# Three of eight channel groups of a depthwise convolution move from VectorE to GpSimd

## The chip, the cores and the metric

The kernel runs on one core of a Trainium2 chip. The metric is the device time of one execution in microseconds (us), as the median of several runs.

## The reference

Two transformer blocks run one after the other on 256 tokens of width 2048, all in float32. The first block is the one that matters here. After a norm and a projection, half of the columns go into a gated, causal depthwise convolution of 1024 channels with 31 taps, and the others into latents for an attention of 8 heads:

```
h = rmsnorm(x, pre_mix_norm);  z = h @ w_in
a, g = split(conv_in);  u = a * sigmoid(g)
u[t, c] = conv_b[c] + sum over j < 31 of conv_w[j, c] * u[t - 30 + j, c]
u = silu(layernorm(u, conv_ln_g, conv_ln_b))
q = rmsnorm(q_lat) @ w_uq;  k, v = rmsnorm(kv_lat) @ w_ukv;  rotary parts;  attn = causal_attention(q, k, v)
mix = concat(rmsnorm(u), rmsnorm(attn)) @ w_out;  x = x + rmsnorm(mix)
x = x + rmsnorm((silu(hf @ w_gate) * (hf @ w_up)) @ w_down),  hf = rmsnorm(x)
```

The second block (window attention, gated linear attention and a convolved feed-forward net) is untouched.

## The kernel before

All weight matrices are streamed from HBM in tiles of 256 rows (two chunks of 128) by up to 512 columns, through a ring of 4 buffers. For each tile ScalarE rounds the weights to a high part (`w_hi`, line 1073), VectorE subtracts to get the low part (`w_lo`, line 1623, both inputs in SBUF), and TensorE multiplies high by high, high by low and low by high (lines 484 to 486): 12 matmuls of up to 512 columns. The rounding of a tile waits until TensorE has used the tile four places earlier; TensorE waits for `lo_ready`, which the subtraction raises. The order of work on every engine is written out by hand: `lo_upto(g)` on VectorE issues the subtractions up to tile g, and other work is put between.

The convolution has its channels on partitions, in 8 groups of 128 (`CC`), with 256 tokens in the free dimension and 30 zeros ahead of them (`uT`). Two halves of the channels become ready at two times: `u_ready`, transposes on TensorE (line 562), and copies out of PSUM on ScalarE (line 1146, `cu_free`). One tap of one group is one VectorE instruction of 128x256, `cv = uT shifted * weight + cv` (line 1729); the first also adds the bias (line 1726). There are 31 x 8 = 248. They are issued by `taps(n)`: 3 behind each of 50 tiles of the input, latent and up projections (`TILE_TAPS`), 12 behind each head of the attention (`ATTN_TAPS`), and the rest ahead of the output projection. The constant `CONV_DVE` lists the groups of each half. With eight groups, four stand in each half.

The attention of the first block has a software pipeline over heads: TensorE transposes q and k of head h+1 (`attn1_T`, lines 607 to 610), makes the scores of head h (`attn1_S`), transposes the weights of head h-1 and makes the product of head h-2. VectorE adds the mask and takes the maximum (lines 1794 to 1797), ScalarE takes exponentials (line 1209), and VectorE scales the output (line 1805). After it TensorE fills the transposed inputs of the output projection (line 500), multiplies two tiles, and then waits for the convolution (`conv_tap`, at g == 2) to sum its columns for the layer norm (line 695).

GpSimd makes constants at the start. After that it takes one power per norm, in the order `R_ORDER` ("x0" the first norm, "lat" the latents, "attn" the attention's), each when VectorE has its mean square: `rstd = ms ** -0.5` (line 465), for which ScalarE waits before it scales the projections' outputs. In the second block it also does rotary products (`rotate`, lines 453 to 458), which read two tensors of SBUF each.

Of the kernel before, what the change touches and what calls it, by code (L numbers as in the profile page):

```python
# [20 lines left out]
F32 = mybir.dt.float32  # L21
F32R = mybir.dt.float32r
I32 = mybir.dt.int32
ALU = mybir.AluOpType
# [3 lines left out]
P = 128  # L28
SEQ = 256
# [10 lines left out]
CC = CONV // P  # L40
TAPS = 31

CONV_DVE = ([0, 1, 2, 3], [4, 5, 6, 7])
TILE_TAPS, ATTN_TAPS = 3, 12
DVE_TAPS = TAPS * sum(len(c) for c in CONV_DVE)
HEADS = 8
NOPE, ROPE, VD = 128, 64, 128
# [2 lines left out]
QC, KVC = QL // P, KVL // P  # L50
# [65 lines left out]
G_AT, _n = {}, 0  # L116
# [7 lines left out]
def build(nc, a, out):  # L124
    ctx = ExitStack()
    with ctx:
# [3 lines left out]
        def overlay(tensors):  # L130

            inner = ExitStack()
            got = [inner.enter_context(nc.sbuf_tensor(n, s, d)) for n, s, d in tensors]
            inner.close()
            return got

        def sem(name):
            return ctx.enter_context(nc.semaphore(name))
# [12 lines left out]
        gains = sb("gains", [P, G_ROWS])  # L151
        convw = sb("convw", [P, TAPS * CC])
# [16 lines left out]
        y_dn, _, grow_dn = overlay([("y_dn", [P, TOK * DM], F32), ("under_grow", [P, DM], F32), ("grow_dn", [P, DM], F32)])  # L169
# [3 lines left out]
        z1, uT, cv, q1, kv1, attn1, qkT, qpeT, att1_s, att1_p, kpe, kpeT = overlay([  # L173
            ("z1", [P, TOK, Z1], F32), ("uT", [P, CC, SEQ + TAPS - 1], F32), ("cv", [P, CC, SEQ], F32),
            ("q1", [P, TOK, HEADS * QKH], F32), ("kv1", [P, TOK, DM], F32), ("attn1", [P, TOK, CONV], F32),
            ("qkT", [P, 2, 2, SEQ], F32), ("qpeT", [ROPE, 2, SEQ], F32), ("att1_s", [P, 2, 3 * P], F32),
            ("att1_p", [P, 2, 3 * P], F32), ("kpe", [P, TOK, ROPE], F32), ("kpeT", [ROPE, SEQ], F32)])
        taken = sum([TOK * Z1, CC * (SEQ + TAPS - 1), CC * SEQ, TOK * HEADS * QKH, TOK * DM, TOK * CONV,
                     4 * SEQ, 2 * SEQ, 6 * P, 6 * P, TOK * ROPE, SEQ])
        _, latT_hi, latT_lo = overlay([("under_lat", [P, taken], F32),  # L180
                                       ("latT_hi", [P, QC + KVC, SEQ], F32R), ("latT_lo", [P, QC + KVC, SEQ], F32R)])
        _, lnsq = overlay([("under_ln", [P, taken], F32), ("lnsq", [P, CC, SEQ], F32)])

        taken = TOK * Z1 + CC * (SEQ + TAPS - 1) + CC * SEQ
        _, grow_out = overlay([("under_gout", [P, taken], F32), ("grow_out", [P, DM], F32)])
        taken += TOK * HEADS * QKH
# [6 lines left out]
        taken = TOK * Z2 + 8 * NB  # L193
# [35 lines left out]
        dve_step, act_step, pool_step = sem("dve_step"), sem("act_step"), sem("pool_step")  # L229
        ms_ready, rstd_ready, sq_done = sem("ms_ready"), sem("rstd_ready"), sem("sq_done")  # L230
        u_ready, cu_ready, cu_free = sem("u_ready"), sem("cu_ready"), sem("cu_free")
        conv_tap = sem("conv_tap")
        trig_arg, trig_abs, trig_done = sem("trig_arg"), sem("trig_abs"), sem("trig_done")
        at_T, at_qk, at_S, at_max, at_exp, at_PT, at_pT, at_PV, at_out = (
            sem("at_T"), sem("at_qk"), sem("at_S"), sem("at_max"), sem("at_exp"), sem("at_PT"), sem("at_pT"),
# [173 lines left out]
        @block.gpsimd  # L409
        def _(pool):  # L410
            count = [0]

            def step(ins):
                count[0] += 1
                ins.then_inc(pool_step, 1)
                pool.wait_ge(pool_step, count[0])

            step(pool.memset(ident[:], 0.0))
            pool.affine_select(out=ident[:], in_=ident[:], compare_op=ALU.not_equal, fill=1.0, base=0,
                               pattern=[[-1, P]], channel_multiplier=1).then_inc(ident_ready, 1)  # L420
            step(pool.memset(masks[:], 0.0))
            step(pool.memset(tri[:], 1.0))

            for at, sign in ((0, 1), (2 * P, 1), (3 * P, -1)):
                step(pool.affine_select(out=masks[:, at:at + P], in_=masks[:, at:at + P], compare_op=ALU.is_ge,
                                        fill=MASKED, base=0, pattern=[[-sign, P]], channel_multiplier=sign))

            for d, (m, c) in enumerate([(-1, 1), (1, -1)]):
                step(pool.affine_select(out=tri[:, d, :], in_=tri[:, d, :], compare_op=ALU.is_ge, fill=0.0,
                                        base=0, pattern=[[c, P]], channel_multiplier=m))  # L430
                step(pool.affine_select(out=tri[:, d, 0:CHUNK], in_=tri[:, d, 0:CHUNK], compare_op=ALU.is_ge,
                                        fill=0.0, base=CHUNK - 1, pattern=[[0, CHUNK]], channel_multiplier=-1))
                step(pool.affine_select(out=tri[:, d, CHUNK:P], in_=tri[:, d, CHUNK:P], compare_op=ALU.is_ge,
                                        fill=0.0, base=-CHUNK, pattern=[[0, CHUNK]], channel_multiplier=1))
            step(pool.tensor_copy(gmask[:], tri[:]))

            step(pool.affine_select(out=gmask[:, 1, :], in_=gmask[:, 1, :], compare_op=ALU.is_gt, fill=0.0,
                                    base=0, pattern=[[-1, P]], channel_multiplier=1))
            pool.iota(posf[:, 1, :], pattern=[[P, TOK]], base=0, channel_multiplier=1,
                      allow_small_or_imprecise_dtypes=True).then_inc(masks_ready, 1)  # L440

            def rotate(part):

                _, h0, n, _, _ = QK_PARTS[part]
                half = HD // 2
                qk = z2[:, :, h0 * HD:(h0 + n) * HD].rearrange("p t (h n) -> p t h n", n=HD)
                x1, x2 = qk[:, :, :, 0:half], qk[:, :, :, half:HD]
                cos, sin = (trig[:, :, i, 32:96].unsqueeze(2).to_broadcast([P, TOK, n, half]) for i in range(2))
                r1, r2, r3, r4 = (gb_flat[:, 1536 + 512 * i:1536 + 512 * i + TOK * n * half]
                                  .rearrange("p (t h n) -> p t h n", t=TOK, n=half) for i in range(4))  # L450
                pool.wait_ge(trig_done, 1)
                pool.wait_ge(qk_normed, part + 1)
                pool.tensor_tensor(r1, x1, sin, ALU.mult)
                pool.tensor_tensor(r2, x2, sin, ALU.mult)
                pool.tensor_tensor(r3, x1, cos, ALU.mult)
                step(pool.tensor_tensor(r4, x2, cos, ALU.mult))
                pool.tensor_tensor(x1, r3, r2, ALU.subtract)
                pool.tensor_tensor(x2, r4, r1, ALU.add).then_inc(rope_ready, 1)
                pool.wait_ge(rope_ready, part + 2)

            pool.wait_ge(consts_ready, 2)
            for n, name in enumerate(R_ORDER):
                pool.wait_ge(ms_ready, n + 1)
                k = R[name][1]
                pool.tensor_tensor(r_of(rstd, name), r_of(ms, name), minus_half[:, 0:k],  # L465
                                   ALU.pow).then_inc(rstd_ready, 1)
                if name in ("k", "qa", "qb", "qc"):
                    rotate([q[0] for q in QK_PARTS].index(name))

# [2 lines left out]
        def _(pe):  # L472
# [216 lines left out]
            for g in range(32):  # L689
                half, b, i = g // 16, g // 4, g % 4  # L690
                if g == 2:
                    pe.wait_ge(conv_tap, DVE_TAPS)
                    pe.wait_ge(tp_free, F_MIX1 + 4)
                    for c in range(CC):
                        mm = pe.matmul(ps[:, 4, 0:SEQ], ones[:], cv[:, c, :], start=(c == 0), stop=(c == CC - 1))
                    mm.then_inc(ln_mm, 1)
                if g == 6:
                    pe.wait_ge(ln_act, 1)
                    column_sums(5)
                if g == 8:  # L700
                    pe.wait_ge(ln_dve, 2)
                    for t in range(TOK):
                        mm = pe.matmul(ps[:, 4, t * P:(t + 1) * P], ones[:], lnsq[:, 0, t * P:(t + 1) * P],
                                       start=True, stop=True)
                    mm.then_inc(ln_mm, 1)
                if g == 14:
                    pe.wait_ge(ln_act, 3)
                    column_sums(5)
                if i == 0 and b < 6:
                    pe.wait_ge(gemm_free[b % 2], 7 + b // 2)  # L710
                if i == 0 and b >= 6:
                    pe.wait_ge(y_ready, 2 * (b - 5))
                if g < 4:
                    pe.wait_ge(tp_free, F_MIX1 + i + 1)
                if 16 <= g < 20:
                    pe.wait_ge(mix_conv, i + 1)
                gemm_tile(T_OUT1 + g, 0, H, CC * (1 - half) + 2 * i, pair(b % 2), i == 0, i == 3)
# [1549 lines left out]
```

## Time and profile before

| | |
|---|---|
| median of 3 runs | 2242.4 us (2240.35 to 2245.7) |
| profiled execution | 2245.7 us, its span 2244.0 us |
| granted TensorE clock, mean | 0.988 |
| TensorE busy | 2196.9 us, 98% |
| VectorE busy | 1294.2 us, 58% |
| ScalarE busy | 1104.9 us, 49% |
| GpSimd busy | 49.8 us, 2% |

The profile is of one execution. Matmuls are pipelined and their ends are modelled, so that 98% does not mean that TensorE is at its peak. In rows, PE is TensorE's matmul, PEld its weight load, DVE is VectorE, ACT ScalarE, POOL GpSimd. L1729 is line 1729 of the kernel.

### The profile page before, as it was taken

How to read it: one execution, taken by the hardware profiler on the slowest of the kernel's cores; microseconds unless marked ns; L12 is line 12 of the kernel's file. 1: busy time of each engine (PE TensorE's matmuls, PEld its weight loads, DVE VectorE, ACT ScalarE, POOL GpSimd, SP SyncE). 2: the span in 40 equal slices, each digit the busy share in tenths (PEclk: the TensorE clock that was granted, in tenths of full speed). 3: DMA queues.
4: the chain of work that ended last, by engine and by line, in shares of the span. 5: the costliest groups of instructions: out<-in, count | busy, mean ns of one | idle time of the engine just before them, and what ended most of it. 6: DMA issues, size and time to landing. Idle time of an engine off the chain costs nothing.

```text
span 2244.0 us, 28723 instructions
## 1 busy us (share of the span) xinstructions
PE 2196.9 (98%) x10142; PEld 1829.1 (82%) x10142; DVE 1294.2 (58%) x1667; ACT 1104.9 (49%) x1443; POOL 49.8 (2%) x59
## 2 busy tenths in 40 slices
PE   8999699999999999999999999999999999999999
PEld 7897587888888888888888877788888888888887
DVE  5798946654455454444465556665565666565443
ACT  5555354544444444444356445546565556554433
POOL 0000000000000000000000013100000000000000
PEclk9999799999999999999999999999999999999999
DMA  7665035566666666655565534456656565656555
GB/s 233 179 186 178 19 113 178 170 187 189 192 189 187 189 190 193 204 189 188 187 173 146 171 112 142 129 177 182 200 175 196 168 201 172 197 177 201 192 188 168
DMA packets 207393, 393.11 MB, mean 175 GB/s; under 512 B 13167, under 2 KB 40889, under 8 KB 207067
## 3 DMA queue, kind: packets, MB, share of 16 engines
q1 hardware_dynamic: 207147, 391.13, 56.8%
q10 hardware_dynamic: 176, 1.06, 0.1%
q8 instruction: 43, 0.70, 0.1%
q14 instruction: 27, 0.22, 0.0%
HBM read 390.04 MB, written 2.10 MB: 175 GB/s over the span
## 4 chain that ended last, share of the span: by engine, by line
PE 93%; DVE 4%; ACT 1%; issue 1%; POOL 0%; DMA 0%; DVEq 0%; ACTq 0%; POOLq 0%
PE ps L484 29%; PE ps L486 29%; PE ps L485 29%; DVE cv L1729 2%; PE ps L500 1%; PE ps L1029 1%; DVE w_lo L1623 1%; PE ps L747 0%; ACT w_hi L1073 0%; PE ps L857 0%; PE ps L876 0%; DVE fac L2018 0%; PE ps L685 0%; PE ps L961 0%; DMA x_sb<-in_x 0%
## 5 line engine op out<-in xcount | busy, mean ns | idle before, releaser
L1623 DVE TENSOR_TENSOR w_lo<-raw,w_hi 128x1024 fp32r<-128x1024 f32 (+2 forms) x761 | 899.1, 1190 | 784.1 <-ACT w_hi L1073 781.0
L1073 ACT ACTIVATE w_hi<-raw 128x1024 fp32r<-128x1024 f32 (+2 forms) x761 | 778.0, 1030 | 738.6 <-PE ps L486 696.1
L484 PE MATMUL ps<-w_hi,hT_hi 128*128 128x512 f32 (+2 forms) x2208 | 868.1, 393 | 12.3 <-DVE w_lo L1623 9.9
L486 PE MATMUL ps<-w_hi,hT_lo 128*128 128x512 f32 (+2 forms) x2208 | 856.5, 388 | 0.0
L485 PE MATMUL ps<-w_lo,hT_hi 128*128 128x512 f32 (+2 forms) x2208 | 856.0, 388 | 0.0
L484 PEld LDWEIGHTS ps<-w_hi,hT_hi 128*128 128x128 f32 x2208 | 417.5, 189 | 97.0 <-issue 9.7
L486 PEld LDWEIGHTS ps<-w_hi,hT_lo 128*128 128x128 f32 x2208 | 417.0, 189 | 80.5
L485 PEld LDWEIGHTS ps<-w_lo,hT_hi 128*128 128x128 f32 x2208 | 418.0, 189 | 76.4
L484 PE MATMUL ps<-w_hi,aT_hi 128*128 128x512 f32 x704 | 274.0, 389 | 0.0
L486 PE MATMUL ps<-w_hi,aT_lo 128*128 128x512 f32 x704 | 273.9, 389 | 0.0
L485 PE MATMUL ps<-w_lo,aT_hi 128*128 128x512 f32 x704 | 273.9, 389 | 0.0
L486 PEld LDWEIGHTS ps<-w_hi,aT_lo 128*128 128x128 f32 x704 | 132.2, 188 | 27.5
L484 PEld LDWEIGHTS ps<-w_hi,aT_hi 128*128 128x128 f32 x704 | 132.2, 188 | 27.5
L485 PEld LDWEIGHTS ps<-w_lo,aT_hi 128*128 128x128 f32 x704 | 132.2, 188 | 27.2
L1729 DVE SCALAR_TENSOR_TENSOR cv<-uT,convw,cv 128x256 f32<-128x256 f32 x240 | 99.7, 477 | 0.0
L1564 ACT ACTIVATE stage<-ps,conv 128x256 f32<-128x256 f32 x88 | 42.5, 563 | 60.0 <-PE ps L1029 60.0
L1097 ACT ACTIVATE hT_hi<-ps,gains 128x256 fp32r<-128x256 f32 x72 | 30.0, 471 | 64.1 <-PE ps L500 64.1
L465 POOL TENSOR_TENSOR rstd<-ms,minus_half 128x2 f32<-128x2 f32 (+2 forms) x15 | 19.5, 1303 | 1458.6 <-DVE ms L1657 1328.7
L1649 DVE SCALAR_TENSOR_TENSOR hT_lo<-ps,gains,hT_hi 128x256 fp32r<-128x256 f32 x72 | 31.4, 479 | 35.0 <-ACT hT_hi L1097 34.9
L1555 ACT ACTIVATE stage<-ps,rstd 128x512 f32<-128x512 f32 x44 | 27.9, 686 | 28.7 <-PE ps L486 28.7
L2192 DVE SCALAR_TENSOR_TENSOR stage<-ps,conv,stage 128x255 f32<-128x255 f32 x88 | 38.1, 475 | 0.0
L2200 DVE SCALAR_TENSOR_TENSOR stage<-ps,conv,stage 128x255 f32<-128x255 f32 x88 | 38.0, 473 | 0.0
(262 smaller groups left out, 1010.2 us busy)
## 6 DMA issues: line engine op xcount, KB each, us to landing
raw<-in_w_up SPq DMA_DIRECT2D x264, 512.0 KB, 4.2
raw<-in_w_down SPq DMA_DIRECT2D x160, 512.0 KB, 4.5
raw<-in_w_gate SPq DMA_DIRECT2D x88, 512.0 KB, 4.4
raw<-in_w_in SPq DMA_DIRECT2D x80, 464.0 KB, 3.6
raw<-in_w_out SPq DMA_DIRECT2D x64, 512.0 KB, 4.2
raw<-in_w_in SPq DMA_DIRECT2D x32, 512.0 KB, 4.5
raw<-in_w_in SPq DMA_DIRECT2D x24, 448.0 KB, 3.4
raw<-in_w_down SPq DMA_DIRECT2D x32, 256.0 KB, 3.0
```

The source lines that it names most:

```text
L484: pe.matmul(o, xh, wh, start=first, stop=False)
L485: pe.matmul(o, xh, wl, start=False, stop=False)
L486: mm = pe.matmul(o, xl, wh, start=False, stop=last)
L1073: act.activation(w_hi[:, s, :kc, :width], raw[:, s, :kc, :width], ACT.Copy).then_inc(hi_ready, 1)
L1097: ins = act.activation(dst[:, k + i, :], ps[:, b, i * SEQ:(i + 1) * SEQ], ACT.Copy, **({"scale": gains[:, at:at + 1]} if gain else {}))
L1555: ins = act.activation(raw_s[:, t, :], ps[:, 2 * half + t, :], ACT.Copy, scale=r_of(rstd, "x3", t, 1))
L1564: ins = act.activation(dst[:, c, :], ps[:, 4 + 2 * half + c // 2, (c % 2) * SEQ:(c % 2 + 1) * SEQ], ACT.Identity, scale=conv2[:, 1, bass.t ...
L1623: dve.tensor_tensor(w_lo[:, s, :kc, :width], raw[:, s, :kc, :width], w_hi[:, s, :kc, :width].bitcast(F32), ALU.subtract).then_inc(lo_ready, 1)
L1649: ins = dve.scalar_tensor_tensor(out=lo[:, k + i, :], in0=src, scalar=gains[:, at:at + 1], in1=h, op0=ALU.mult, op1=ALU.subtract)
L1729: ins = dve.scalar_tensor_tensor(out=cv[:, c, :], in0=u, scalar=w, in1=cv[:, c, :], op0=ALU.mult, op1=ALU.add)
L2192: ins = dve.scalar_tensor_tensor(out=dst[:, c, 1:SEQ], in0=src[:, 0:SEQ - 1], scalar=conv2[:, 0, bass.ts(k, 1)], in1=dst[:, c, 1:SEQ], op0 ...
L2200: ins = dve.scalar_tensor_tensor(out=dst[:, c, 0:SEQ - 1], in0=src[:, 1:SEQ], scalar=conv2[:, 2, bass.ts(k, 1)], in1=dst[:, c, 0:SEQ - 1], ...
```

## The change

Group lists are cut: VectorE keeps groups 0, 1 and 4, 5, 6; GpSimd gets 2, 3 and 7. Each of its taps is a product into a scratch tile `tap_prod` and a sum, each waiting for the one before. It does its groups of a half at once, so its instructions are 128x512 in the first half and 128x256 in the second. The first pass is put into its queue behind the power for "x0", the second behind the power for "lat". `ATTN_TAPS` becomes 4, and TensorE's column sums wait for GpSimd's sums too.

```diff
-CONV_DVE = ([0, 1, 2, 3], [4, 5, 6, 7])
-TILE_TAPS, ATTN_TAPS = 3, 12
+CONV_DVE = ([0, 1], [4, 5, 6])
+CONV_POOL = ([2, 3], [7])
+TILE_TAPS, ATTN_TAPS = 3, 4
...
+        taken += 2 * (QC + KVC) * SEQ
+        _, tap_prod = overlay([("under_tap", [P, taken], F32), ("tap_prod", [P, 2, SEQ], F32)])
...
+            def pool_conv(g):
+                c, k, base = CONV_POOL[g][0], len(CONV_POOL[g]), (TAPS - 1) * g
+                acc, prod = cv[:, c:c + k, :], tap_prod[:, 0:k, :]
+                def tap(out, j):
+                    w = convw[:, bass.ds(j * CC + c, k)].unsqueeze(2).to_broadcast([P, k, SEQ])
+                    return pool.tensor_tensor(out, uT[:, c:c + k, bass.ds(j, SEQ)], w, ALU.mult)
+                pool.wait_ge(gains_ready, 3)
+                pool.wait_ge(cu_free, 2 * g + 2)
+                step(tap(acc, 0))
+                at = G_AT["conv_b"] + c
+                bias = gains[:, at:at + k].unsqueeze(2).to_broadcast([P, k, SEQ])
+                step(pool.tensor_tensor(acc, acc, bias, ALU.add))
+                with pool.Fori(0, (TAPS - 1) // 6) as r:
+                    for i in range(1, 7):
+                        tap(prod, 6 * r + i).then_inc(pool_mul, 1)
+                        pool.wait_ge(pool_mul, base + 6 * r + i)
+                        pool.tensor_tensor(acc, acc, prod, ALU.add).then_inc(pool_add, 1)
+                        pool.wait_ge(pool_add, base + 6 * r + i)
...
+                if name in ("x0", "lat"):
+                    pool_conv(0 if name == "x0" else 1)
...
                     pe.wait_ge(conv_tap, DVE_TAPS)
+                    pe.wait_ge(pool_add, 2 * (TAPS - 1))
```

## Rows read from the trace of the kernel before

**Rows 1.** The page's chain that ended last, shares by line

```profile
PE ps L484 29%; PE ps L486 29%; PE ps L485 29%; DVE cv L1729 2%; PE ps L500 1%; PE ps L1029 1%; DVE w_lo L1623 1%; PE ps L747 0%; ACT w_hi L1073 0%; PE ps L857 0%; PE ps L876 0%; DVE fac L2018 0%; PE ps L685 0%; PE ps L961 0%; DMA x_sb<-in_x 0%
```

**Rows 2.** The chain in order of time: start us, duration us, engine, tile, line

```profile
71.02 0.87 PE ps L562 x8
...
114.29 0.88 PE ps L562 x8
154.08 1.31 PE ps L500 x12
...
275.05 3.68 PE ps L500 x16
```

**Rows 3.** Busy us (instructions) in stretches: PE, PEld, DVE, ACT, POOL, clock, DMA, GB/s

```profile
77.00:117.00 40.00, 40.00 (x188) 34.39 (x187) 36.82 (x65) 19.62 (x22) 0.00 (x0) 1.00 0.67 186
171.00:216.00 45.00, 42.81 (x194) 34.75 (x193) 38.38 (x70) 24.64 (x34) 1.23 (x1) 1.00 0.55 176
223.00:275.00 52.00, 32.61 (x151) 25.86 (x150) 51.48 (x149) 15.07 (x48) 0.00 (x0) 0.74 0.05 22
```

**Rows 4.** VectorE's groups, 77 to 171 us (two rows), then 223.2 to 275

```profile
L1729 DVE SCALAR_TENSOR_TENSOR cv<-uT,convw,cv 128x256 f32<-128x256 f32 x104 | 44.1, 478 | 0.0
L1623 DVE TENSOR_TENSOR w_lo<-raw,w_hi 128x896 fp32r<-128x896 f32 x24 | 26.1, 1087 | 6.6 <-ACT w_hi L1073 6.4
...
L1729 DVE SCALAR_TENSOR_TENSOR cv<-uT,convw,cv 128x256 f32<-128x256 f32 x97 | 39.0, 476 | 0.0
```

**Rows 5.** Timeline (start, duration, idle before): copy, subtraction, and power for the latents

```profile
71.49 1.09 ACT L1146 ACTIVATE uT<-ps 128x512 f32<-128x512 f32 x2 [2.04 <-PE ps L562]
...
75.74 1.22 DVE L1623 TENSOR_TENSOR w_lo<-raw,w_hi 128x1024 fp32r<-128x1024 f32 x1 [2.62 <-ACT w_hi L1073]
...
170.31 1.92 POOL L465 TENSOR_TENSOR rstd<-ms,minus_half 128x4 f32<-128x4 f32 x1 [129.79 <-DVE ms L1750]
```

**Rows 6.** Timeline of GpSimd in the second block

```profile
1321.69 0.73 POOL L455 TENSOR_TENSOR gb<-z,trig 128x256 f32<-128x256 f32 x1
1322.39 1.61 POOL L456 TENSOR_TENSOR gb<-z,trig 128x256 f32<-128x256 f32 x1
...
1352.13 1.28 POOL L454 TENSOR_TENSOR gb<-z,trig 128x512 f32<-128x512 f32 x1
1353.36 2.15 POOL L455 TENSOR_TENSOR gb<-z,trig 128x512 f32<-128x512 f32 x1
1355.47 1.28 POOL L456 TENSOR_TENSOR gb<-z,trig 128x512 f32<-128x512 f32 x1
1356.83 1.30 POOL L457 TENSOR_TENSOR z<-gb 128x512 f32<-128x512 f32 x1
```

**Rows 7.** Timeline of VectorE beside these, and of both engines at 1400 us

```profile
1321.88 1.53 DVE L1623 TENSOR_TENSOR w_lo<-raw,w_hi 128x928 fp32r<-128x928 f32 x1 [1.46 <-ACT w_hi L1073]
...
1325.33 2.20 DVE L1623 TENSOR_TENSOR w_lo<-raw,w_hi 128x928 fp32r<-128x928 f32 x2
...
1352.31 2.08 DVE L1623 TENSOR_TENSOR w_lo<-raw,w_hi 128x928 fp32r<-128x928 f32 x1
...
1399.83 1.37 DVE L1623 TENSOR_TENSOR w_lo<-raw,w_hi 128x1024 fp32r<-128x1024 f32 x1 [1.29 <-ACT w_hi L1073]
1401.12 0.69 DVE L2141 TENSOR_TENSOR asum<-asum,amax 128x2 f32<-128x2 f32 x1
...
1400.08 1.72 POOL L455 TENSOR_TENSOR gb<-z,trig 128x256 f32<-128x256 f32 x1
```

**Rows 8.** Timeline at the start of the attention, heads 1 to 4

```profile
223.22 0.14 PEld L607 LDWEIGHTS ps<-ident,q 128*128 128x128 f32 x1
226.91 0.14 PEld L607 LDWEIGHTS ps<-ident,q 128*128 128x128 f32 x1
...
223.04 0.56 DVE L1794 TENSOR_TENSOR att_s<-ps,masks 128x384 f32<-128x384 f32 x1 [1.29 <-PE ps L623]
...
225.29 0.19 ACT L1209 ACTIVATION_READ_ACCUMULATOR att_s<-att_s,amax 128x1 f32 x1
```

More of the change, by code:

```diff
@@ L231, in build @@
         u_ready, cu_ready, cu_free = sem("u_ready"), sem("cu_ready"), sem("cu_free")
-        conv_tap = sem("conv_tap")
+        conv_tap, pool_mul, pool_add = sem("conv_tap"), sem("pool_mul"), sem("pool_add")
         trig_arg, trig_abs, trig_done = sem("trig_arg"), sem("trig_abs"), sem("trig_done")
```

## The prediction

> **What bounds the kernel now.** I read the shares of the chain of waits first, then the chain in order of time, then the busy time of stretches, and last the single instructions of VectorE and GpSimd. The chain [rows 1] is nearly all TensorE, by the three matmul lines; the convolution's line 1729 on VectorE is the only other group worth its name, 2%. The chain in order of time [rows 2] says where those 2% lie. Up to 216 us TensorE sets the pace: three of its events stand 16 tiles apart, 71.02 to 114.29 and 114.29 to 154.08, which is 2.70 and 2.49 us a tile. In the first attention, 223 to 275 us, VectorE sets it [rows 3]: busy 51.48 of 52 us, 97 taps among its work [rows 4], while TensorE is busy 32.61 and its granted clock has sunk to 0.74, a mixture of its two levels. So taps that leave the attention are worth time.
>
> The same rows show what the change leans on. Before the attention VectorE is nearly full too: 36.82 of 40 us in 77 to 117, 38.38 of 45 us in 171 to 216 [rows 3]. A tile costs it one low-part subtraction and three taps. The subtraction takes 1.09 us for a 448-column tile [rows 4] and 1.22 for 512 [rows 5], a tap 0.48; but they overlap a little, and back to back a tap takes 0.40 (39.0 us for 97, [rows 4]), so a tile costs 2.2 to 2.4 us against 2.5 to 2.7 of TensorE. Anything that adds more than 0.3 us to a tile there stops TensorE.
>
> **The change, part by part.** *Removed from VectorE*: channel groups 2, 3 and 7, 93 of 248 taps. The three taps behind each tile stay (50 places, 150 taps), so of the 155 left only 5 fall into the attention, where there were 98. Nothing is relieved before 216 us: the same number of taps stands behind each tile.
>
> *What the attention gains.* Without taps the pace is TensorE's. Head 3's transposes begin at 223.22 and head 4's at 226.91 [rows 8], a period of 3.69 us in which TensorE found its inputs ready. From the mask of head 1 (223.04) six more periods reach the mask of head 7, 22.1 us; its softmax to the end of its exponentials is 2.4 us (223.04 to 225.48 for head 1, [rows 8]), and I allow as much again for transpose, copy, product and scaling: 250.0 against 275.05 us, where TensorE takes up the fills [rows 2]. That is 25 us gained. The price if the clock stays at the 0.74 of [rows 3]: a period of 3.69/0.74 = 5.0, 8 us less, 17 gained. The five taps left (2 us) lie beside the first two heads.
>
> *Added on GpSimd*: two passes. The first, on two channel groups at once, starts when the gated input is copied out, 72.6 us [rows 5], and has 1 product, 1 bias and 30 times product and sum: 62 instructions of 128x512. The second has 62 of 128x256 and stands behind the latents' power, at 170.3 us before [rows 5]. GpSimd was idle, so its time by itself costs nothing: alone such an instruction takes 1.28 and about 0.73 us [rows 6], and with 0.08 us for the wait between dependent ones (1355.47+1.28 to 1356.83, [rows 6]) the passes would take 62 x 1.36 = 84 and 62 x 0.81 = 50 us, both within the room before their deadlines.
>
> *What they cost VectorE.* Here the trace speaks against the change. In the second block GpSimd's rotations meet VectorE's subtractions, and each holds up the other. VectorE's subtraction at 1352.31 takes 2.08 us, where two in a row take 2.20 (1.12 and 1.08 behind it, the row at 1325.33): it ends 0.98 after GpSimd's product at 1352.13 does (1353.41). GpSimd's next product, started at 1353.36, takes 2.15 instead of 1.28 us and ends 1.12 after the subtraction [rows 6, 7]. The end of one GpSimd product to the end of the next is 2.10 us, of which the subtraction alone would be 1.08: one GpSimd instruction of 128x512 pushes VectorE by 1.02. The same for 128x256: ends at 1322.42 and 1324.00, 1.58 apart, less 1.08: 0.50 us [rows 6, 7]. And the turn changes even when VectorE has its next instruction ready: at 1401.12 a sum of two elements, next in the queue behind a subtraction, takes 0.69 us and ends at 1401.81, just as GpSimd's product does that was waiting since 1400.08 and went first (1401.80, [rows 7]). The taps read two tensors of SBUF as the subtractions do. No row has a tap beside a GpSimd instruction; I take them like the subtraction, their nearest row, and keep a free pass for them as a rival. [...]
>
> With VectorE full, each GpSimd instruction pushes it by its price, whichever way the turns fall. Low bound 1.02 and 0.50; high bound 1.36 and 0.81, GpSimd's pace alone with the wait, if VectorE could use none of the gaps. Since a tap of 0.40 us hides less of GpSimd's start and finish than a subtraction does, I take 1.10 and 0.60.
>
> First pass: 62 x 1.10 = 68. Off it goes what was idle: 2.6 us before the subtraction at 75.74 (for which VectorE waited 2.62, [rows 5]), 3.2 us in 77 to 117 [rows 3], and VectorE's lead over TensorE, done with that tile at 76.96 where TensorE reaches it at about 71.02+0.87+4x2.6 = 82.3, 5.3 us. 68-11 = 57 us. It spans only some 15 tiles, each 4 turns of VectorE and 4 of GpSimd, about 6.6 us, so TensorE waits in most. The clock may halve there, but 5.2 us for a tile is still under 6.6, and costs nothing.
>
> Second pass: 62 x 0.60 = 37, less 6.6 us of idle VectorE in 171 to 216 [rows 3] and 3 us of lead: 27 us. A tile is then 4.5 us of VectorE; a slow clock (5.2) would add up to 0.7 on 14 tiles, 10 us, kept for the high end.
>
> *Order on GpSimd's queue.* Behind the first pass is the power for the latents, behind the second that for the attention norm. The first ends near 72.6 + 62 x 1.7 = 178 us (1.10 plus about 0.6, a mean turn of VectorE), the latents are then not due before 170+57 = 227. The second runs from 227 to about 300, the attention then ends near 326, and the column sums that wait for it come later still. Both waits are met, so I cost them at nothing; a longer loop overhead on GpSimd would eat this cover of 25 to 50 us first. Bias, semaphores and the scratch tile have no other price.
>
> Sum: +57 +27 -25 = **+59 us**. The profiled execution took 2245.7 us around its span of 2244.0, hence 2304.7 in its terms; it is the slowest of the three before, 3.3 over the median. On the median: 2242.4 + 59 = **2301 us**, 2.6% slower.
>
> **The rivals.**
> (1) *Only the subtractions are held up, the taps pass.* Then the sign turns. A tile has one subtraction, which meets GpSimd's reading on most tiles and waits part of 1.02; a mean of 0.4 gives 2.8 us a tile against 2.5 to 2.7, over 36 tiles 7 us; GpSimd gets about 1.4 instructions into a tile, so a dozen are left when the latents are due, some 10 us; the second pass costs 3. 20-25 = -5: 2237 us, faster by 0.2%. It decides from less than about 0.4 us a GpSimd instruction on average. Against it: the taps have the same kind of operands as what is seen blocked.
> (2) *VectorE's queue keeps its turn; GpSimd gets in only where VectorE pauses.* Then VectorE hardly slows, but GpSimd gets perhaps 30 of 62 instructions in before the latents are due, and 32 x 1.36 = 44 us are waited for at their power; the second pass slides into the attention, where there is room. With 15 us for the turns it does get: +44+15-25 = +34: 2276 us. Against it stands the row at 1401.12.
> (3) *No contention that matters*: the change does just what it says, -25: 2217 us. Against it, every row of GpSimd beside a subtraction.
> (4) *GpSimd's loop is slower than its rows*, by over 0.5 us an instruction (register waits): the power for the latents comes late by tens of us, and the second pass delays the column sums: 59 + 30 = +89: 2331 us.
>
> **How the numbers follow.** Forecast 0.70, (1) 0.10, (2) 0.10, (3) 0.03, (4) 0.07. The forecast's own range: 62 x 1.02 - 11 + 62 x 0.50 - 10 - 25 = +48 (rounded: 52+21-25), to 84 - 11 + 50 - 7 - 17 = +99, thus 2290 to 2341. The range takes in most of (2) and (4): 2264 to 2343. Three runs of before lie 5 us apart, so 0.2%, 4.5 us, is about what can be told from no change. Slower: 0.70+0.10+0.07 = 0.87, less a little for a sum mis-sized in several terms: 0.85. Faster takes rival 3, 0.03, and most of rival 1, whose time lies at the very edge: 0.10. Same has the rest, 0.05.
>
> **What would show it.** Right: taps and subtractions before the attention stretched to 1.4 to 2.3 us; GpSimd's 128x512 products alternating with them, 1.5 to 2.3 us from one to the next; TensorE waiting for the low parts from about 80 to 180 us, tiles some 6 us apart, at a lower clock; a second, weaker such stretch after 227 us; attention from first mask to fills in 27 us instead of 52, with almost no taps. Each step has its own mark: where GpSimd's rows grow but taps don't, it is rival 2; where only line 1623 grows, rival 1; a wait of the scaling for the latents' power points to rival 4. The prediction is wrong if a tap's turn takes much less than a subtraction's, or the attention finds another chain when the taps are gone, for then the 25 us are less.

## The result: slower by 1.75%

The changed kernel takes 2282.56 us in the median of four runs (2280.47 to 2286.49), the kernel before 2242.73 (2240.35 to 2245.7): a ratio of 1.0175, 95% interval 1.0163 to 1.0188, or 40 us. Forecast were 59 us, 2301, with a range of 2264 to 2343. The profiled execution took 2285.92 us around a span of 2284.2, 40.2 over the span before.

The chain that ended last, shares by line, in the page of the changed kernel (its line 1759 is 1729 of before, 1653 is 1623, 529 is 500):

```profile
PE ps L513 28%; PE ps L515 27%; PE ps L514 27%; DVE cv L1759 4%; DVE w_lo L1653 3%; PE ps L1059 1%; PE ps L529 1%; PE ps L777 0%; PE ps L887 0%; DMA raw<-in_w_in 0%; PE ps L906 0%; ACT w_hi L1103 0%; PE ps L652 0%; DVE fac L2048 0%; PE ps L714 0%
```

The taps' share went up from 2 to 4% though 93 of 248 are gone from VectorE, and the subtractions' from 1 to 3% [rows 1]. The chain in order of time says where:

```profile
79.58 2.24 DVE w_lo L1653
81.83 3.01 DVE cv L1759 x3
84.83 1.98 DVE w_lo L1653
86.81 3.02 DVE cv L1759 x3
...
100.05 2.22 DVE w_lo L1653
...
200.01 1.31 PE ps L529 x12
...
257.01 1.67 DVE w_lo L1653
258.68 2.02 DVE cv L1759 x3
...
271.56 1.68 DVE w_lo L1653
...
317.25 1.97 PE ps L529 x16
```

From about 80 us the path is no longer TensorE's but VectorE's. Four tiles take 20.47 us (79.58 to 100.05), 5.1 each, where TensorE needed 2.7; the three taps behind one take 3.0 us instead of 1.2. The latents' fills on line 529 come at 200.01, before 154.08 [rows 2]: 45.9 us late, and this is the first pass. In the second pass four tiles take 14.55 us, 3.6 each. The mask of head 1 starts at 285.48 (223.04 before, [rows 8]), 62.4 late: 16.5 more. The fills behind the attention start at 317.25 (275.05), so that the attention gave 20.2 us back. Until the end of the program 2.0 more come back, 1.0 of them in the first tiles behind those fills (column sums 8.3 us behind, before 9.3), where the clock before was still at 0.51 (275 to 279 us) and the change's is at 1.00 (317 to 327). 45.9+16.5-20.2-2.0 = 40.2.

Busy time in stretches of the changed kernel (columns as in [rows 3]): the middle of the first pass, the attention, and two parts of it:

```profile
77.00:117.00 40.00, 30.67 (x107) 21.83 (x106) 40.00 (x32) 11.50 (x13) 35.10 (x25) 0.87 0.35 100
...
284.00:317.00 33.00, 28.54 (x150) 21.53 (x150) 18.75 (x62) 16.32 (x52) 5.22 (x7) 0.81 0.14 48
...
281.00:296.00 15.00, 11.83 (x39) 8.25 (x38) 11.00 (x25) 5.65 (x19) 7.81 (x9) 0.50 0.20 70
296.00:317.00 21.00, 19.18 (x117) 14.28 (x116) 10.76 (x40) 10.67 (x34) 0.00 (x0) 0.99 0.15 51
```

In 77 to 117 us VectorE is busy for all 40 us and gets 32 instructions done, before 65 in 36.82 [rows 3]: over half of its busy time is waiting inside the instruction. In the attention it is busy 18.75 of 33 us, before 51.48 of 52.

The clock has two levels in these traces, 0.50 and 1.00. The 0.74 of the kernel before in its attention [rows 3] is a mixture of them: of 104 slices of 0.5 us in 223 to 275 us, 44 read 1.00 and 49 read 0.50, and the other 11 lie between. A stretch of before at each level:

```profile
223.00:231.00 8.00, 6.73 (x41) 4.85 (x40) 7.82 (x23) 3.62 (x12) 0.00 (x0) 1.00 0.02 7
259.00:268.00 9.00, 4.37 (x21) 4.08 (x20) 8.93 (x26) 1.97 (x6) 0.00 (x0) 0.50 0.00 0
```

The changed kernel's VectorE instructions in 77 to 171 us (count, busy us, mean ns, idle before):

```profile
L1759 DVE SCALAR_TENSOR_TENSOR cv<-uT,convw,cv 128x256 f32<-128x256 f32 x54 | 56.3, 1093 | 0.0
L1653 DVE TENSOR_TENSOR w_lo<-raw,w_hi 128x896 fp32r<-128x896 f32 x10 | 20.6, 2060 | 0.0
L1653 DVE TENSOR_TENSOR w_lo<-raw,w_hi 128x1024 fp32r<-128x1024 f32 x8 | 17.4, 2179 | 0.0
```

A tap is 1093 ns in the mean instead of 478, a narrow subtraction 2060 instead of 1087 [rows 4]. GpSimd's side, in order of time:

```profile
72.09 1.04 POOL L453 TENSOR_TENSOR cv<-uT,convw 128x512 f32<-128x512 f32 x1 [32.23 <-ACT uT L1176]
73.22 1.04 POOL L460 TENSOR_TENSOR cv<-cv,gains 128x512 f32<-128x512 f32 x1
...
85.81 2.15 POOL L465 TENSOR_TENSOR cv<-cv,tap_prod 128x512 f32<-128x512 f32 x1
88.25 1.29 POOL L453 TENSOR_TENSOR tap_prod<-uT,convw 128x512 f32 x1 [0.28 <-POOL cv L465]
...
216.24 1.93 POOL L492 TENSOR_TENSOR rstd<-ms,minus_half 128x4 f32<-128x4 f32 x1 [40.95 <-DVE ms L1780]
...
221.05 0.62 POOL L453 TENSOR_TENSOR tap_prod<-uT,convw 128x256 f32 x1 [0.73 <-POOL cv L460]
221.75 0.74 POOL L465 TENSOR_TENSOR cv<-cv,tap_prod 128x256 f32<-128x256 f32 x1
```

The sum at 85.81 waits for the subtraction of 84.83. A product alone takes 1.04 us and 0.62, less than the 1.28 and 0.73 of the rotations [rows 6]. Ahead of each product in the loop 0.28 us pass, and 0.54 where a turn of the loop begins; ahead of each sum, 0.08. The power for the latents, at 216.24, had waited 40.95 us for its input, so GpSimd's queue was not late.

### The profile page after: what moved, and what is told of

Same layout as the page of the kernel before. It is cut to its first block, busy times and chain, and to the rows that moved or that the text cites. A ratio compares the mean times of both kernels' runs of the same rounds, so it can differ in the third digit from the quotient of the medians.

```text
span 2284.2 us, 28928 instructions
## 1 busy us (share of the span) xinstructions
PE 2216.1 (97%) x10142; PEld 1833.4 (80%) x10142; DVE 1334.8 (58%) x1574; ACT 1104.4 (48%) x1443; POOL 200.8 (9%) x183
## 4 chain that ended last, share of the span: by engine, by line
PE 88%; DVE 9%; ACT 1%; issue 0%; DMA 0%; POOL 0%; SPq 0%; DVEq 0%; ACTq 0%; POOLq 0%
PE ps L513 28%; PE ps L515 27%; PE ps L514 27%; DVE cv L1759 4%; DVE w_lo L1653 3%; PE ps L1059 1%; PE ps L529 1%; PE ps L777 0%; PE ps L887 0%; DMA raw<-in_w_in 0%; PE ps L906 0%; ACT w_hi L1103 0%; PE ps L652 0%; DVE fac L2048 0%; PE ps L714 0%
## 5 line engine op out<-in xcount | busy, mean ns | idle before, releaser
L1653 DVE TENSOR_TENSOR w_lo<-raw,w_hi 128x1024 fp32r<-128x1024 f32 (+2 forms) x761 | 924.1, 1223 | 773.2 <-ACT w_hi L1103 769.6
L1759 DVE SCALAR_TENSOR_TENSOR cv<-uT,convw,cv 128x256 f32<-128x256 f32 x150 | 110.5, 787 | 0.0
L465 POOL TENSOR_TENSOR cv<-cv,tap_prod 128x512 f32<-128x512 f32 (+1 forms) x60 | 79.3, 1321 | 4.7
L453 POOL TENSOR_TENSOR tap_prod<-uT,convw 128x512 f32 (+1 forms) x60 | 67.3, 1122 | 19.7 <-POOL cv L465 18.6
```

Of the source, the lines that this page charges most:

```text
L453: return pool.tensor_tensor(out, uT[:, c:c + k, bass.ds(j, SEQ)], w, ALU.mult)
L465: pool.tensor_tensor(acc, acc, prod, ALU.add).then_inc(pool_add, 1)
L1653: dve.tensor_tensor(w_lo[:, s, :kc, :width], raw[:, s, :kc, :width], w_hi[:, s, :kc, :width].bitcast(F32), ALU.subtract).then_inc(lo_ready, 1)
L1759: ins = dve.scalar_tensor_tensor(out=cv[:, c, :], in0=u, scalar=w, in1=cv[:, c, :], op0=ALU.mult, op1=ALU.add)
```

## Experiments

All times are beside runs of the kernel before on the same chip. In the four sets of runs the kernel before had a median between 2242.7 and 2244.2 us, so ratios compare better than times. I call an attention's length the time from the mask of head 1 to the fills: 52.0 us before, 31.8 changed.

**The change without GpSimd's loop.** The first product and the bias of each pass stay.

```diff
-                with pool.Fori(0, (TAPS - 1) // 6) as r:
-                    ...
-                    pe.wait_ge(pool_add, 2 * (TAPS - 1))
+                    pe.wait_ge(pool_step, 18)
```

> The changed kernel without GpSimd's 30 products and 30 sums in each pass (its first product and the bias stay), so the convolution lacks these taps of groups 2, 3 and 7. It has the relief of VectorE's attention without GpSimd's work. Theory A (each GpSimd instruction that reads SBUF holds VectorE's taps and subtractions up; 0.93 us for 128x512 and 0.44 us for 128x256, as the changed kernel's rows give it): all of the loss is gone and the attention runs at TensorE's pace with its clock at full: 52 us from the mask of head 1 to the fills become 27, the time is 2218 us (2215 to 2222). Theory B (the loss is in the order of the taps on VectorE or in the new wait before the column sums, not in GpSimd's work): above 2235 us.

2215.71 us, ratio 0.9872 (0.9853 to 0.9891). Theory A holds: the whole loss is GpSimd's loop. One thing was missed: the attention took 30.1 us in the profile, not 27, for the clock was not at full. Two stretches of that profile:

```profile
221.00:233.00 12.00, 12.00 (x40) 8.39 (x39) 5.19 (x17) 4.98 (x17) 0.00 (x0) 0.50 0.14 44
233.00:256.00 23.00, 20.93 (x129) 15.86 (x128) 12.01 (x44) 11.43 (x36) 0.00 (x0) 0.98 0.13 47
```

**GpSimd as busy, but only writing.** The loop is written out, and each of its instructions is a pair of memsets; groups 2, 3 and 7 become zero.

```diff
-                        tap(prod, 6 * r + i).then_inc(pool_mul, 1)
+                        pool.memset(acc, 0.0)
+                        pool.memset(prod, 0.0).then_inc(pool_mul, 1)
...
-                        pool.tensor_tensor(acc, acc, prod, ALU.add).then_inc(pool_add, 1)
+                        pool.memset(acc, 0.0)
+                        pool.memset(prod, 0.0).then_inc(pool_add, 1)
```

> The changed kernel with each product and each sum of the loop replaced by two memsets of the same tile (128x512 and 128x512, or 128x256 twice), which read nothing, with the same semaphores; groups 2, 3 and 7 of the convolution become zero. GpSimd is busy about as long, some 1.0 us where a product took 1.04 alone. Theory A (the loss is a blocked read): VectorE's instructions keep 0.48 and 1.1 to 1.2 us, the time is that of the run without the loop, about 2218 us (to 2224). Theory C (any GpSimd instruction blocks VectorE, its writes as well, or being busy is what costs): VectorE's taps stretch as in the changed kernel, 2265 to 2285 us.

2214.81 us, ratio 0.987 (0.9852 to 0.9888), the same as without a loop. Groups of GpSimd in the whole span (one of eight alike), and of VectorE in 76 to 171 us:

```profile
L464 POOL MEMSET tap_prod<- 128x512 f32 x30 | 16.1, 536 | 0.0
...
L1761 DVE SCALAR_TENSOR_TENSOR cv<-uT,convw,cv 128x256 f32<-128x256 f32 x103 | 43.6, 475 | 0.0
L1655 DVE TENSOR_TENSOR w_lo<-raw,w_hi 128x896 fp32r<-128x896 f32 x24 | 26.1, 1086 | 6.3 <-ACT w_hi L1105 6.3
```

240 memsets kept GpSimd busy and VectorE's taps and subtractions have their old 475 and 1086 ns. So for these instructions it is neither that GpSimd works, nor its writes, nor its semaphores: what stretched them to 1093 and 2060 ns in the change is its reading. The attention took 26.1 us here, with the clock at full (1.00 in 223 to 249 us).

**One tensor read instead of two.** Loop written out; products and sums become copies of the shifted input into the scratch tile, and groups 2, 3 and 7 lack 30 taps.

```diff
-                        tap(prod, 6 * r + i).then_inc(pool_mul, 1)
+                        pool.tensor_copy(prod, uT[:, c:c + k, 6 * r + i:6 * r + i + SEQ]).then_inc(pool_mul, 1)
...
-                        pool.tensor_tensor(acc, acc, prod, ALU.add).then_inc(pool_add, 1)
+                        pool.tensor_copy(prod, uT[:, c:c + k, 6 * r + i:6 * r + i + SEQ]).then_inc(pool_add, 1)
```

> The loop written out, and each product and sum replaced by a copy of the same part of the input into the scratch tile: one tensor read instead of two; groups 2, 3 and 7 lack 30 taps. Theory A (the hold is of the read interface, for as long as GpSimd reads): it still blocks, for the copy's shorter reading, some 0.4 us for 128x512 and 0.2 for 128x256: passes at 15 and 3 us instead of 46 and 16, time 2230 to 2248 us. Theory G (only GpSimd instructions with two SBUF inputs block VectorE): 2215 us, as with the memsets.

2235.37 us, ratio 0.9959 (0.9944 to 0.9974), inside theory A's range; the latents' fills came at 168.42, 14 us late. VectorE, then GpSimd, in order of time:

```profile
82.83 1.63 DVE L1653 TENSOR_TENSOR w_lo<-raw,w_hi 128x1024 fp32r<-128x1024 f32 x1
84.38 2.33 DVE L1759 SCALAR_TENSOR_TENSOR cv<-uT,convw,cv 128x256 f32<-128x256 f32 x3
86.64 1.62 DVE L1653 TENSOR_TENSOR w_lo<-raw,w_hi 128x1024 fp32r<-128x1024 f32 x1
...
83.44 1.49 POOL L463 COPY tap_prod<-uT 128x512 f32<-128x512 f32 x1
84.99 0.69 POOL L465 COPY tap_prod<-uT 128x512 f32<-128x512 f32 x1
85.75 0.69 POOL L463 COPY tap_prod<-uT 128x512 f32<-128x512 f32 x1
86.50 0.69 POOL L465 COPY tap_prod<-uT 128x512 f32<-128x512 f32 x1
```

Turn by turn: four copies to four instructions of VectorE, every tile. The tile takes 3.81 us, of which VectorE's own work is 1.13+3x0.40 = 2.33, so a copy pushes it by 0.37 us. One tensor read by GpSimd is enough to block. Of the read interface that theory A names, the rows show these turns and no more.

**The loop written out.** Nothing else changes.

> The changed kernel with GpSimd's loop written out, so that the 0.28 us ahead of each product (waits against a register) become about 0.08. Theory A (VectorE is full, so each GpSimd instruction pushes it by its hold whichever way the turns fall): the passes are shorter, but the pushes stay: 2282 us (2278 to 2288). Theory F (the gaps let VectorE's taps through for nothing, which is why an instruction cost 0.93 and 0.44 and not 1.02 and 0.50): without them 60 times 0.1 to 0.2 us more, 2288 to 2294 us.

2285.4 us, ratio 1.0183 (1.0168 to 1.0199), not to be told from the change. GpSimd's first pass ended 10 us sooner (its last sum starts at 163.05, against 173.27), and TensorE's fills came at 200.44 against 200.01. A tile of VectorE, and GpSimd beside it:

```profile
86.61 2.06 DVE L1653 TENSOR_TENSOR w_lo<-raw,w_hi 128x1024 fp32r<-128x1024 f32 x1
88.59 4.11 DVE L1759 SCALAR_TENSOR_TENSOR cv<-uT,convw,cv 128x256 f32<-128x256 f32 x3
92.62 2.05 DVE L1653 TENSOR_TENSOR w_lo<-raw,w_hi 128x1024 fp32r<-128x1024 f32 x1
...
87.66 2.15 POOL L465 TENSOR_TENSOR cv<-cv,tap_prod 128x512 f32<-128x512 f32 x1
89.89 1.10 POOL L453 TENSOR_TENSOR tap_prod<-uT,convw 128x512 f32<-128x512 f32 x1
91.08 1.34 POOL L465 TENSOR_TENSOR cv<-cv,tap_prod 128x512 f32<-128x512 f32 x1
92.49 1.10 POOL L453 TENSOR_TENSOR tap_prod<-uT,convw 128x512 f32<-128x512 f32 x1
```

Now four GpSimd instructions start in a tile, as many as VectorE's own, and the tile takes 6.01 us; with the gaps of the loop it was three and 5.1 us. A push is (6.01-2.33)/4 = 0.92 us. With VectorE full the number of pushes counts, not how densely they come; theory F, which wanted a higher price, is out. The mask of head 1 came at 288.22, 2.7 us behind the change's: the last sum started at 279.73, ahead of the attention, whereas five of the change's instructions start behind that mask.

**Each pass alone.** Group 7 back to VectorE (the first two lines with a plus), or groups 2 and 3 (the last two); the pass left out and its wait go too.

```diff
-CONV_DVE = ([0, 1], [4, 5, 6])
-TILE_TAPS, ATTN_TAPS = 3, 4
+CONV_DVE = ([0, 1], [4, 5, 6, 7])
+TILE_TAPS, ATTN_TAPS = 3, 5
...
+CONV_DVE = ([0, 1, 2, 3], [4, 5, 6])
+TILE_TAPS, ATTN_TAPS = 3, 9
```

> Only groups 2 and 3 go to GpSimd; VectorE keeps group 7 (186 taps, 36 of them in the attention, 5 behind a head). Theory A with separate prices: the first pass costs 46 us as in the changed kernel, 16 tiles of it at 5.1 us; the second stretch is as before; the attention still runs at TensorE's pace, since 4.5 taps of 0.40 us fit into the 1.86 us that VectorE has left of each head, and it starts at full clock: -25. Sum 2242.7+46-25 = 2264 us (2260 to 2268). Theory D (most of the loss comes from the second pass, which delays the latents' power and meets the attention): below 2250 us.

2266.25 us, ratio 1.0102 (1.0085 to 1.012). The mask of head 1 came 47.1 us late (270.12), and the attention was 22.6 shorter (29.4).

> Only group 7 goes to GpSimd, behind the latents' power; VectorE has 217 taps, 67 of them in the attention (9 behind a head). Theory A: the pass costs 16 us before the attention and the attention loses 31 taps of 0.40 us, 12.5: 2247 us (2243 to 2251). Theory D: above 2265 us.

2248.06 us, ratio 1.0023 (1.0011 to 1.0035). The mask of head 1 came 15.9 us late (238.96). The attention was 10.2 shorter (41.8), not 12.5; four GpSimd instructions still started in it. Both prices, 46 and 16 us, are right and theory D is out. Even the cheaper pass costs more than its taps gave back.

**The second pass in the attention.** As the last, and GpSimd waits for the first transposes (`pool.wait_ge(at_T, 1)`).

> As the run with only the second pass, but GpSimd waits until the attention's first transposes. Theory A: the 10 us of idle VectorE that hid part of the pass before the attention are gone, and in the attention VectorE is full with 67 taps: 62 x 0.44 = 27 us of pushes, of which the masks and maxima, with at most one SBUF tensor as second input, take no part, against 16 before; so 2252 to 2260 us where the same work ahead of it took 2248. Theory H (the attention has room on the port, since its own VectorE work reads PSUM): below 2246 us.

2247.66 us, ratio 1.0019 (1.001 to 1.0029): between the two theories. The attention took 57.2 us, 5.2 more than before with 31 taps fewer, so the pushes came to 12.5+5.2 = 17.7, or 0.32 for each of the 56 GpSimd instructions that start in it. VectorE in 222 to 285 us:

```profile
L1760 DVE SCALAR_TENSOR_TENSOR cv<-uT,convw,cv 128x256 f32<-128x256 f32 x67 | 42.2, 697 | 0.0
...
L1825 DVE TENSOR_TENSOR att_s<-ps,masks 128x384 f32<-128x384 f32 x7 | 3.8, 546 | 0.4 <-PE ps L653 0.4
...
L1828 DVE TENSOR_SCALAR amax<-amax 128x2 f32<-128x2 f32 x8 | 3.2, 395 | 0.3
L1827 DVE TENSOR_REDUCE amax<-att_s 128x1 f32<-128x256 f32 x7 | 2.9, 409 | 0.0
L1826 DVE TENSOR_REDUCE amax<-att_s 128x1 f32<-128x128 f32 x7 | 2.0, 287 | 0.2
```

The taps are stretched to 697 ns (476 before). The mask sums, which read PSUM and SBUF, are not stretched at all (546 here, 549 before), nor are the maxima, which read one tensor of SBUF (409 and 287 here, 409 and 286 before): these take no part, as theory A said. The scaling of the maxima behind them (line 1828) reads one tensor of SBUF too and takes 395 ns instead of 169, so the count of SBUF inputs alone does not settle who is held up; and the port of theory H is in no row. GpSimd had free turns beside the mask sums and the maxima, more than I gave it, but no room that would have paid.

**VectorE less full beside the passes.** The change with 2 taps instead of 3 behind tiles 24 to 35 and 63 to 76 (`taps(TILE_TAPS - 1)`).

> The changed kernel with 2 taps of VectorE instead of 3 behind tiles 24 to 35 and 63 to 76, so that 31 instead of 5 are left for the attention. Theory A (VectorE is full beside GpSimd's passes, and the attention, paced by TensorE at 3.69 us a head against 1.83 of VectorE, has room for 4 taps a head): 26 taps of 0.40 us come off the path and cost nothing in the attention: 2282.6-10 = 2272 us (2269 to 2277). If GpSimd simply takes the turns that come free, the time stays: 2280 us or more.

2267.62 us, ratio 1.0108 (1.009 to 1.0125), some 15 us under the change and 1.4 under the range of theory A. The mask of head 1 came at 270.51 instead of 285.48, 15.0 sooner, for 10.4 us of taps. A tile of VectorE, and GpSimd beside it:

```profile
81.98 2.05 DVE L1653 TENSOR_TENSOR w_lo<-raw,w_hi 128x1024 fp32r<-128x1024 f32 x1
83.96 1.90 DVE L1759 SCALAR_TENSOR_TENSOR cv<-uT,convw,cv 128x256 f32<-128x256 f32 x2
85.78 2.06 DVE L1653 TENSOR_TENSOR w_lo<-raw,w_hi 128x1024 fp32r<-128x1024 f32 x1
...
83.03 2.15 POOL L465 TENSOR_TENSOR cv<-cv,tap_prod 128x512 f32<-128x512 f32 x1
85.47 1.30 POOL L453 TENSOR_TENSOR tap_prod<-uT,convw 128x512 f32 x1 [0.29 <-POOL cv L465]
```

VectorE is as full as before, and the price is the old one: the tile takes 3.80 us, VectorE's own work is 1.13+2x0.40 = 1.93, and two GpSimd instructions start in it, 0.94 us each. What changed is where the pushes fall. Fourteen instructions of the second pass start behind the mask of head 1, against five in the change; at 0.44 these nine are 4.0 us. The first pass spans some four tiles more, for the latents' fills (193.96) come 14.6 us behind its end and not 24.7; a narrow tile takes TensorE 2.49 us and VectorE alone 2.19 (184.56 to 186.75 in this profile), which is 0.3 of room in each, or 1.2. Together that is 5.2 us, where 4.6 are left to explain: an estimate, which no run took apart. The sum of theory A had left both out. The attention took 30.4 us against the change's 31.8, but that does not make its pushes free: its clock was at 0.94 in the mean, and the change's at 0.50 for its first 10.5 us.

**No GpSimd, better packing.** The kernel before with a fourth tap behind wide tiles, in the loops over tiles 24 to 35 and 63 to 76; `ATTN_TAPS` is 10.

```diff
-                taps(TILE_TAPS)
+                taps(TILE_TAPS + (g < 32))
...
-                taps(TILE_TAPS)
+                taps(TILE_TAPS + 1)
```

> The kernel before, without any tap on GpSimd, but with 4 taps instead of 3 behind the 22 tiles that are 512 columns wide from tile 24 on, so that 76 instead of 98 are left for the attention. TensorE takes 2.7 us for such a tile, VectorE 1.14+4x0.40 = 2.74. If the attention's length is VectorE's (6.65 us a head with 12 taps), 22 taps less are 8.8 us less, and the tiles lose 22 x 0.05 to 0.1 = 1 to 2 us: 2236 us (2233 to 2239). If VectorE's room before the attention is already used up, the 8.8 us come back there: 2243 us.

2234.89 us, ratio 0.9961 (0.9948 to 0.9975). Then all 50 tiles with four taps (`TILE_TAPS, ATTN_TAPS = 4, 6`):

> The kernel before with 4 taps behind each of the 50 tiles, so that 48 are left for the attention (6 behind a head: 1.83+2.4 = 4.2 us of VectorE a head against 3.69 of TensorE). Against the run with 4 behind the wide tiles: 28 taps less in the attention, 11 us; but the narrow tiles take VectorE 1.00+1.60 = 2.6 us against 2.5 of TensorE, 3 us lost on 24 of them and their neighbours. 2227 us (2223 to 2232). If the room before the attention is used up, 2235 us or more.

2227.18 us, ratio 0.9923 (0.991 to 0.9936): 17 us faster than before and 55 faster than the change. Of the kernels that leave no work out only the next is as fast. Two stretches of its profile, 77 to 117 us and the attention:

```profile
77.00:117.00 40.00, 40.00 (x189) 34.38 (x188) 40.00 (x76) 19.64 (x22) 0.00 (x0) 1.00 0.62 172
...
227.00:261.00 34.00, 26.60 (x153) 20.06 (x152) 32.56 (x100) 15.16 (x50) 0.00 (x0) 0.90 0.11 39
```

Now VectorE is full at both places, with 76 instructions in those 40 us (65 before, 32 changed), and TensorE still gets its tiles. The mask of head 1 came 4.4 us later than before, the attention took 33.5 instead of 52.0.

**The same with TensorE kept busy at the attention's start.** `keep_warm(6, 6)` ahead of its first transposes, `keep_warm(6, 7)` behind them.

> The same with two groups of 6 small matmuls on TensorE in its waits at the attention's start, ahead of the first transposes and behind them. In several profiles the granted clock was 0.5 for 11 to 13 us there, which cost 5 to 6 us against a profile without it. If TensorE's pauses just before are what lets the clock fall, 3 to 5 us less than without them, 2223 us; if not, 1 us more, 2228 us.

2226.37 us, ratio 0.9923 (0.991 to 0.9936): no difference. The fall that the expectation speaks of is in the profile of the change (0.50 in 281 to 296 us, attention 31.8 us) and in the one without the loop (0.50 in 221 to 233, 30.1 us); against 26.1 us at 1.00 with the memsets that is 5.7 and 4.0 us. But the profile without these matmuls had the clock at 1.00 in 223 to 239 us too, so there was no fall at the attention's start for them to prevent. Later, in 239 to 262 us, where TensorE waits for VectorE, the clock was at 0.72 with them and 0.84 without. What sets it was not settled.

## Why the prediction was right, and where it was off

*What bounds it* was right: VectorE's 36.82 of 40 us were the row that decided, since any push there is a push of TensorE (busy 40.00 of 40 us in 77 to 117 before, 30.67 with the change). "Up to 216 us TensorE sets the pace" is too broad: in about 191 to 203 us the chain of before runs over ScalarE and VectorE, with the rotary sums and the taps behind them. The sum does not rest on it.

*The blocking* was right, for the taps too, of which no row was there before: 1093 ns in the mean. The run with memsets (475 ns a tap) and the one of copies (0.37 us a push) show that it is GpSimd's reading. Rival 1 (taps pass), rival 2 (GpSimd gets only pauses) and rival 3 (no contention) fall by these rows: GpSimd alternated with queued taps and subtractions, and in the run of copies and the one with the loop written out exactly one to one.

*The price of a push* is the term that was mis-sized: 1.10 and 0.60 us were forecast. In the 20.47 us of four tiles in the first pass GpSimd starts 12 instructions, and VectorE's own work is 4 x 2.33 = 9.32: (20.47-9.32)/12 = 0.93 us. In the second, (14.55-9.32)/12 = 0.44. I had raised the bounds of 1.02 and 0.50, measured against subtractions, by my own estimate that a tap hides less of GpSimd's start and finish, which no row shows; and I took the rotary product for the nearest row, while the product with one weight per partition is shorter (1.04 against 1.28 us). Neither the raise nor the 1.02 held. The shorter product is nearly the whole of what the bounds missed: with every second instruction 0.24 and 0.12 us shorter they would be 0.90 and 0.44 (an estimate). The other runs give the same price whether two, three or four GpSimd instructions fall into a tile: 0.94, 0.93 and 0.92. With the measured prices the sum's own way gives 62x0.93-11 = 46.7 and 62x0.44-9.6 = 17.7, against 45.9 and 16.5 read from the chain: the 11 and 9.6 us taken off for idle time and lead were about right, and so was the count of 62. This one term is some 10 of the 57 us and 10 of the 27. The tile of some 6 us, with four turns of each engine, came only with the loop written out; the gaps of the loop made it three turns and 5.1 us.

*The attention* gained 20.2 us where 25 was said. Its path was right: with the clock at full (the memsets) it took 26.1 us, 25.9 less than before. The period of 3.69 us is there: masks of heads 4 and 5 in the changed kernel start at

```profile
301.57 0.56 DVE L1824 TENSOR_TENSOR att_s<-ps,masks 128x384 f32<-128x384 f32 x1 [1.69 <-PE ps L652]
...
305.27 0.56 DVE L1824 TENSOR_TENSOR att_s<-ps,masks 128x384 f32<-128x384 f32 x1 [1.69 <-PE ps L652]
```

with VectorE now waiting for TensorE. But in 281 to 296 us the clock was granted at 0.50, the lower of its two levels, behind a second pass in which TensorE was busy 44.22 of 56 us (228 to 284). The prediction had that as the low price of 17 us. Runs without a pass in the way show both sizes: 26.1 us with the clock at full (the memsets) and 30.1 with twelve microseconds at 0.50 (no loop). In the run without a loop no pass had starved TensorE (busy 42.53 of 45 us in 171 to 216, the memsets' 42.52), and one fell to 0.50 and the other did not: that starving leads to it was not shown.

*The number* owes something to luck. The passes cost 45.9+16.5 = 62.4 us where 84 was said, 21.6 too much; the attention gave 4.8 less than said, and 2.0 came back behind it. The two errors have opposite signs, and the 59 missed the 40.2 by 18.8 us and not by 23.6.

*The order on GpSimd's queue* cost nothing, as said; rival 4 falls. The passes ended sooner than I had reckoned (the first at 175, not 178 us). The gap ahead of a product is 0.28 us in the loop instead of 0.08, and by the written-out loop the time does not depend on it. What makes it was not separated: the wait ahead of each sum is against a register too and shows 0.08, while only the products take their addresses from the loop's register.

## What to carry to other kernels

Before moving work from VectorE to GpSimd, look whether VectorE's instructions read two tensors of SBUF, whether GpSimd's read even one, and whether VectorE is full at that time. Where all three held here, they took turns (taps at 1093 and narrow subtractions at 2060 ns instead of 478 and 1087; 0.37 us a copy of one tensor): one tap of 0.40 us of VectorE became two GpSimd instructions that took 2x0.44 from it, so the move lost at each of the places where it was tried. Price such a move by the number of GpSimd instructions and their own rows, not by their nearest relative's. Turns that cost VectorE nothing were those beside its mask sums, which read PSUM (546 ns against 549), and its maxima (409 and 287 against 409 and 286); a stage that is full of one engine's filler is better relieved by packing the same filler into the tiles that still have tenths of a microsecond left.

## What was not expected of the hardware

- GpSimd's product with a weight that is one element per partition and group is faster than the rotary product, whose table changes from element to element: 1.04 against 1.28 us for 128x512, 0.61 to 0.62 against 0.73 for 128x256. It is not the operation: adding the bias, also one element, takes 1.04 and 0.61, and the sum of two full tensors 0.74 for 128x256.
- 240 memsets of GpSimd beside VectorE left its two-input instructions at 475 and 1086 ns, while the 60 copies of 128x512, which read one tensor, held it up by 0.37 us each.
- The memsets did hold up one kind of VectorE's instructions: the first taps (`TENSOR_SCALAR`, one tensor of SBUF), 0.41 us without the loop, took 0.69 in the median of five and up to 0.75 beside them. So that GpSimd only writes made it harmless to the two-input instructions, not to all.
- In GpSimd's loop 0.28 us pass ahead of a product and 0.08 ahead of a sum, though the wait ahead of each is against a register; written out, it is 0.08 ahead of both.
